# A hybrid encoder's beginning rebuilt: X loaded and turned by token blocks, parameters turned later

## What is computed

```
h    = x * rsqrt(mean(x*x) + eps) * g_mix_pre
proj = h @ w_in            # q1 q2 k1 k2 v lru_x lru_gate gate_attn gate_lru
lam  = exp(sum(lq1*lk1)) - exp(sum(lq2*lk2)) + lam_init      # used by the attention
a    = exp(-8 * r_gate * softplus(-lru_lambda))              # decay, used by the recurrence
```

## Time and profile before

| what | us |
|---|---|
| median of 3 runs | 2166.58 |
| lowest, highest | 2165.35, 2169.26 |
| the profiled execution, its own time | 2163.76 |
| its span, first to last instruction | 2161.6 |
| first row load issued, first product of the trio | 0.75, 39.41 |
| trio from, to | 39.41, 66.11 |

### The profile page before, as it was taken

How to read it: one execution, slowest core, us unless ns; L and a number is a source line. 1 busy time by engine, 2 the same in 40 slices (tenths; PEclk the granted TensorE clock), 3 DMA queues, 4 the chain that set the end, 5 groups by cost and what they waited for, 6 DMA issues and landing times.

```text
span 2161.6 us, 39635 instructions
## 1 busy us (share of the span) xinstructions
PE 2066.7 (96%) x15925; PEld 2013.3 (93%) x15925; DVE 1078.6 (50%) x2102; ACT 956.5 (44%) x1573; POOL 255.8 (12%) x283
## 2 busy tenths in 40 slices
PE   4999999999999899999989999999999989999997
PEld 4899999998999899999979999999999979999997
DVE  3366666665445432243455666666554363223434
ACT  4346464647235441233353656565652353312324
POOL 1303030200020220021012111111001102001200
PEclk9999999999999999999999999999999999999999
DMA  3313131312332223333322222222222323233332
GB/s 98 102 50 102 50 102 50 92 50 69 88 88 69 82 85 88 88 88 88 88 69 83 69 82 66 86 64 78 69 70 87 88 69 88 79 87 88 88 89 70
DMA packets 308155, 172.05 MB, mean 80 GB/s; under 512 B 7296, under 2 KB 303568, under 8 KB 308016
## 3 DMA queue, kind: packets, MB, share of 16 engines
q1 hardware_dynamic: 300720, 155.47, 24.9%
q0 software_dynamic: 7232, 14.49, 2.4%
q10 hardware_dynamic: 64, 0.13, 0.0%
HBM read 158.86 MB, written 11.21 MB: 79 GB/s over the span
## 4 chain that ended last, share of the span: by engine, by line
PE 81%; DVE 8%; ACT 7%; issue 3%; DMA 1%; ACTq 0%; DVEq 0%
PE PJ L529 60%; PE PJ L672 5%; PE PJ L541 4%; PE PX L698 3%; PE PX L736 3%; DVE w_lo L1356 2%; ACT w_hi L920 2%; PE PX L541 1%; DVE s L1558 1%; PE PX L546 1%; PE PX L714 1%; PE PX L624 1%; PE PX L692 1%; DVE uc L1595 1%; ACT L946 0%
## 5 line engine op out<-in xcount | busy, mean ns | idle before, releaser
L1356 DVE TENSOR_TENSOR w_lo<-w_raw,w_hi 128x1024 fp32r<-128x1024 f32 x288 | 385.5, 1351 | 360.7 <-ACT w_hi L920 360.1
L529 PE MATMUL PJ<-h_hi,w_hi 128*128 128x272 f32 x2304 | 491.0, 295 | 17.6 <-DVE w_lo L1356 16.7
L529 PE MATMUL PJ<-h_lo,w_hi 128*128 128x272 f32 x2304 | 475.9, 288 | 0.0
L529 PE MATMUL PJ<-h_hi,w_lo 128*128 128x272 f32 x2304 | 475.3, 288 | 0.0
L920 ACT ACTIVATE w_hi<-w_raw 128x1024 fp32r<-128x1024 f32 x288 | 298.4, 1047 | 209.8 <-DMA w_raw<-in_w_down 115.7
L529 PEld LDWEIGHTS PJ<-h_hi,w_hi 128*128 128x128 f32 x2304 | 362.9, 190 | 22.7 <-issue 12.4
L529 PEld LDWEIGHTS PJ<-h_hi,w_lo 128*128 128x128 f32 x2304 | 362.6, 189 | 0.0
L529 PEld LDWEIGHTS PJ<-h_lo,w_hi 128*128 128x128 f32 x2304 | 361.9, 189 | 0.0
L529 PE MATMUL PJ<-u_hi,w_hi 128*128 128x272 f32 x960 | 198.0, 288 | 3.4 <-DVE w_lo L1356 3.4
L529 PE MATMUL PJ<-u_lo,w_hi 128*128 128x272 f32 x960 | 197.8, 287 | 0.0
L529 PE MATMUL PJ<-u_hi,w_lo 128*128 128x272 f32 x960 | 197.3, 287 | 0.0
(11 more groups left out here) (293 smaller groups left out, 3761.9 us busy)
## 6 DMA issues: line engine op xcount, KB each, us to landing
w_raw<-in_w_in SPq DMA_DIRECT2D x112, 512.0 KB, 3.8
w_raw<-in_w_up SPq DMA_DIRECT2D x64, 512.0 KB, 4.0
w_raw<-in_w_down SPq DMA_DIRECT2D x64, 512.0 KB, 3.6
w_raw<-in_w_branch_attn SPq DMA_DIRECT2D x16, 512.0 KB, 3.6
w_raw<-in_w_branch_lru SPq DMA_DIRECT2D x16, 512.0 KB, 3.6
w_raw<-in_w_out SPq DMA_DIRECT2D x16, 512.0 KB, 3.6
out_prompt_k<-stage POOLq DMA_DIRECT2D x16, 256.0 KB, 2.8
out_prompt_v<-GA POOLq DMA_DIRECT2D x8, 512.0 KB, 3.9
```

Of the source, the lines that this page charges most:

```text
L529: mm = pe.matmul(PJ[:, buf, half, 0:HT], w[a], src[b][:, k0 + k, HT * half:HT * half + HT], start=first and k == 0 and a + b == 0, stop=en ...
L1356: dve.tensor_tensor(w_lo[:, n.slot, :, :], w_raw[:, n.slot, :, :], w_hi[:, n.hi, :, :].bitcast(F32), ALU.subtract).then_inc(w_lo_ready, 1)
```

## The change

- SP loads x_sample, blocks 1 and 2 of x_prompt (128 tokens each, 512 KB), weight tiles 0 and 1, blocks 3 and 4, weight tiles 2 and 3. Each block has its own semaphore.
- ACT's first load is the first norm's gain of layer 0, as 8 rows of 128 values, which PE turns by itself into `first_gain`; `h_chunk(0, ...)` and `h_rest(0, ...)` use that instead of `par`. ACT keeps four of the 13 row loads; the other nine move to POOL's queue, ahead of the fill of `w_gate` and of the lambda loads.
- PE turns X by token block: the sample block, block 1, the gain, block 2; blocks 3 and 4 inside the trio's first half, after k = 0 and k = 2; the parameter rows after k = 7. A block takes two PSUM banks; ACT copies one (feature tiles 0 to 3) into X, DVE the other.
- ACT loads the Exp table first. Splits of weight tiles, pieces of h and squares alternate, in the order in which the trio asks for them. The fourth split, the decay chain and the lambda products come behind h.
- POOL's first load of past keys waits for the last copy on DVE instead of for the last on ACT.
- The counts of `x_new` lose the 8 of the beginning; the rest of the kernel is the same.

```diff
 @@ SP
-            sp.dma_start(x_in[:, 1:5, :], A["x_prompt"][0].rearrange("(g t) d -> t g d", t=P)).then_inc(x_landed, 16)
+            for g in range(3):
+                load_x(g)
             for i in range(WR):
                 sp.dma_start(w_raw[:, i, :, :], pair_source(0, 0, i)).then_inc(w_landed[i], 16)
+                if i == 1:
+                    load_x(3)
+                    load_x(4)
 @@ POOL
+            for row, name in SMALL[4:]:
+                load_small(pool, row, name, small_landed)
+            for l in range(DEPTH):
+                pool.dma_start(rows[16 * l + R_CW:16 * l + R_CW + 4, :], A["conv_w"][l]).then_inc(small_landed, 16)
+                pool.dma_start(rows[16 * l + R_SC:16 * l + R_SC + 3, :], A["state_conv"][l, 0]).then_inc(small_landed, 16)
             pool.memset(w_gate[:], 0.0).then_inc(wg_zero, 1)
 @@ PE
+            def turn_x(g):
+                pe.wait_ge(x_landed[g], 16)
+                if g == 4:
+                    pe.wait_ge(x_in_dve, 1)
+                    pe.wait_ge(gain_ready, 1)
+                for b in range(2):
+                    for k in range(4):
+                        mm = pe.transpose(x_bank(g, b)[:, P * k:P * k + P], x_in[:, g, P * (4 * b + k):P * (4 * b + k) + P], ident[:])
+                    mm.then_inc(x_turned, 1)
+            def turn_par():
+                pe.wait_ge(par_landed, 16 * 4)
+                pe.wait_ge(small_landed, 16 * (5 + 2 * DEPTH))
+                pe.wait_ge(x_in_act, 4)
+                pe.wait_ge(x_in_dve, 5)
+                for k in range(KT):
+                    mm = pe.transpose(PX[:, 1, 32 * k:32 * k + 32], rows[0:32, P * k:P * k + P], ident[0:32, 0:32])
+                mm.then_inc(par_turned, 1)
 @@ PE, trio
+                        if S == 0 and h == 0 and k in (0, 2):
+                            turn_x(3 + k // 2)
+                        if S == 0 and h == 0 and k == KT - 1:
+                            turn_par()
+                        if S == 0 and h == 1 and k == 5:
+                            pe.wait_ge(par_step, 1)
 @@ PE, beginning
-            pe.wait_ge(par_landed, 16 * PAR_DMAS)
...
-            pe.wait_ge(x_new, KT)
+            pe.wait_ge(x_landed[0], 16)
...
+            turn_x(1)
+            pe.wait_ge(gain_landed, 16)
+            pe.transpose(PX[:, 1, 0:KT], gain_row[:], ident[0:KT, 0:KT]).then_inc(gain_turned, 1)
+            turn_x(2)
 @@ ACT, beginning
+            act.dma_start(gain_row[:], A["g_mix_pre"][0].rearrange("(k p) -> k p", p=P)).then_inc(gain_landed, 16)
+            for row, name in SMALL[:4]:
+                load_small(act, row, name, par_landed)
+            act.wait_ge(lam_step, 1)
+            load_table(ACT.Exp)
+            place_x(1)
+            place_x(2)
+            split_hi(pair_tile(0, 0, 0))
+            h_chunk(0, 0, 0)
+            h_chunk(0, 0, 1)
+            split_hi(pair_tile(0, 0, 1))
+            h_chunk(0, 0, 2)
+            place_x(3)
+            h_chunk(0, 0, 3)
+            h_chunk(0, 0, 4)
+            split_hi(pair_tile(0, 0, 2))
+            place_x(4)
+            x_chunk_square(0, 0)
...
+            act.wait_ge(par_step, 2)
             act.activation(lsc[:, 1, :], lsc[:, 0, :], ACT.Exp, scale=-1.0).then_inc(lam_act, 1)
+            split_hi(pair_tile(0, 0, 3))
+            for c in range(5):
+                x_chunk_square(1, c)
             act.wait_ge(lam_step, 4)
             act.activation(lsc[:, 7, 0:4], lsc[:, 6, 0:4], ACT.Exp).then_inc(lam_act, 1)
...
-            load_table(ACT.Ln)
-            for i in range(WR):
-                split_hi(pair_tile(0, 0, i))
 @@ DVE, beginning
+            place_x(0)
+            place_x(1)
+            dve.wait_ge(gain_turned, 1)
+            dve.tensor_copy(first_gain[:], PX[:, 1, 0:KT]).then_inc(gain_ready, 1)
+            place_x(2)
+            split_lo(pair_tile(0, 0, 0))
+            h_rest(0, 0, 0)
+            h_rest(0, 0, 1)
+            split_lo(pair_tile(0, 0, 1))
+            h_rest(0, 0, 2)
+            place_x(3)
+            h_rest(0, 0, 3)
+            h_rest(0, 0, 4)
+            place_x(4)
+            split_lo(pair_tile(0, 0, 2))
...
+            dve.wait_ge(par_turned, 1)
+            dve.tensor_copy(par[:], PX[:, 1, 0:256].rearrange("p (k r) -> p k r", r=32)).then_inc(par_step, 1)
...
+            split_lo(pair_tile(0, 0, 3))
             dve.wait_ge(lam_landed, 16 * 5 * DEPTH)
```

More of the change, by code:

```diff
@@ L275, in x_count @@
         def x_count(S):
[L277 removed]
+            return 10 * (S - 1)
         def x_whole(S):
[L281 removed]
+            return 10 * S
         def squares(l, s):
@@ L313, in proj, with pre_gain, x_bank, load_small @@
             return PJ[:, n.slot % 2, :, 0:HT]
+        def pre_gain(S, k):
+            return first_gain[:, k:k + 1] if S == 0 else gain(S // 2, k, R_MPRE if S % 2 else R_GPRE)
+        def x_bank(g, b):
+            return PX[:, b, :] if g == 4 else PX[:, 2 + b, :] if g == 3 else PJ[:, g - 1, b, :]
         def gain(l, k, row):
             return par[:, k, 16 * l + row:16 * l + row + 1]
+        SMALL = [(row, name) for row, name in (
+            (R_GPRE, "g_mix_pre"), (R_GPOST, "g_mix_post"), (R_MPRE, "g_mlp_pre"), (R_MPOST, "g_mlp_post"),
+            (R_CB, "conv_b"), (R_BR, "b_rg"), (R_BI, "b_ig"), (R_LAM, "lru_lambda"), (R_SL, "state_lru"))]
+        def load_small(eng, row, name, landed):
+            eng.dma_start(rows[row:row + 16 * (DEPTH - 1) + 1:16, :],
+                          A[name].rearrange("l o d -> (l o) d") if name == "state_lru" else A[name]).then_inc(landed, 16)
         def columns(name, l, block):
@@ L1173, in down_end, with place_x @@
                 f_square(l, 7, 0)
[L1176 to L1181, removed]
+            def place_x(g):
+                act.wait_ge(x_turned, 2 * g)
+                act.activation(X[:, 0:4, cols(g)], x_bank(g, 0).rearrange("p (k c) -> p k c", k=4), ACT.Copy).then_inc(x_in_act, 1)
@@ L1711, in _, with place_x @@
             dve.memset(dist_p[0:CHUNK, NP_ - CHUNK:NP_], NEG_DIST)
[L1713 to L1724, removed]
+            def place_x(g):
+                if g == 0:
+                    dve.wait_ge(x_turned, 1)
+                    dve.tensor_copy(X[:, :, 0:NS], PX[:, 0, 0:256].rearrange("p (k c) -> p k c", k=KT)).then_inc(x_in_dve, 1)
+                    return
+                dve.wait_ge(x_turned, 2 * g + 1)
+                dve.tensor_copy(X[:, 4:8, cols(g)], x_bank(g, 1).rearrange("p (k c) -> p k c", k=4)).then_inc(x_in_dve, 1)
+            place_x(0)
[13 more added lines that the diff above has]
+            split_lo(pair_tile(0, 0, 2))
+            h_rest(0, 1, 0)
+            h_rest(0, 1, 1)
+            h_rest(0, 1, 2)
+            h_rest(0, 1, 3)
             dve.wait_ge(par_turned, 1)
-            dve.tensor_copy(par[:], PX[:, 0, 0:256].rearrange("p (k r) -> p k r", r=32)).then_inc(par_step, 1)
+            dve.tensor_copy(par[:], PX[:, 1, 0:256].rearrange("p (k r) -> p k r", r=32)).then_inc(par_step, 1)
             dve.wait_ge(par_step, 1)
+            h_rest(0, 1, 4)
             for l in range(DEPTH):
@@ L1747, in _ @@
             dve.tensor_scalar(lsc[:, 2, :], lsc[:, 2, :], 0.0, None, ALU.max).then_inc(par_step, 1)
+            split_lo(pair_tile(0, 0, 3))
+            dve.wait_ge(lam_landed, 16 * 5 * DEPTH)
+            for l in range(DEPTH):
+                for j in range(2):
+                    i = dve.tensor_tensor_reduce(out=lprod[:], in0=lq[:, l, 2 * j, :], in1=lq[:, l, 2 * j + 1, :], scale=1.0, scalar=0.0,
+                                                 op0=ALU.mult, op1=ALU.add, accum_out=lsc[:, 6, 2 * l + j:2 * l + j + 1])
+                    if l == DEPTH - 1 and j == 1:
+                        i.then_inc(lam_step, 1)
+                    else:
+                        i.then_inc(lambda_chain, 1)
+                        dve.wait_ge(lambda_chain, 2 * l + j + 1)
+            for l in range(DEPTH):
+                dve.tensor_scalar(gs[:, l:l + 1], gs[:, l:l + 1], 1.0 - lam_init[l], None, ALU.mult)
             dve.wait_ge(lam_act, 1)
```

77 lines of the change are left out of this document (35 added, 42 removed).

## The result

| what | before | after |
|---|---|---|
| median, us | 2166.45 | 2144.52 |
| lowest, highest | 2165.35, 2169.26 | 2144.22, 2145.51 |
| profiled execution, own time | 2163.76 | 2144.52 |
| its span | 2161.6 | 2142.7 |
| trio from, to | 39.41, 66.11 | 13.16, 44.21 |

The changed kernel is faster: ratio 0.9898, 95% interval [0.988, 0.9915], 21.9 us by the medians. The forecast was 2145.0 us.

A forecast was written before the change was run, and what follows sets the result against it. PE's wait for thirteen row loads, then chained copies and splits, bounded the beginning. Trio's end from 66.1 to 44.5, 21.6 us less, gave 2142.2; with the 2.8 distance to the median, 2145.0 us; range 2140.5 to 2153.

The forecast's parts named there:

- The bound: Kernel's beginning: PE waits for all thirteen parameter row loads, until 20.93 us, not for X or the weights.
- Loads: Queues at start: bytes over measured pace plus 1.7 us; block 1 at 6.3, tile 1 at 12.0, no wait on SP.
- Until the second tile: Beginning, bounded by the chain of copies and splits: first product at 13.2 us, second tile's at 14.9.
- The trio: First three weight tiles: third stalls 0.3 us for VectorE; end at 44.5 instead of 66.1, 21.6 us less.
- Covers: Work under the trio's second half costs nothing: VectorE done near 40, lambda landed by about 24.7, PE asks at 44.5.
- Pieces paying one after another: Rival, start loads: each load pays its whole 3.8 us behind the one before; gain 16.0, 2150.6 us; chance 0.13.
- PE staying slow: Rival, trio's first half: fast product spacing comes only with the second half; gain 13.9, 2152.7 us; chance 0.11.
- Lambda too late: Rival, slower, before first rs product: lambda loads behind nine POOL loads cost from landing about 35; 62 gives 2171; chance 0.03.
- The path not shortened: Rival, trio: its length set by something keeping its time, as tiles 2 and 3 landing; gain below 4 us; chance 0.03.
- none of the gain is lost there: Stage behind the trio (66.11 to 78.58): waits counted from the trio's end, so the 21.6 us gain passes through.
- a sign of being wrong: Stages behind the trio: forecast wrong if they differ by more than 1 us, or if the trio ends after 53.
- The distance of span to median: Whole kernel: median 2166.58 stands 2.8 us above the profiled execution; kept, turning 2142.2 into 2145.0 us.

The follow-up runs named there:

- the trial: Changed kernel with the lambda and g_sub loads issued only when the trio's first half is done; 2144.58 us, ratio 0.9896.
- the disturbed landing above: Changed kernel unedited, measured and profiled a second time, its third weight tile landing at 22.49 us; 2146.34 us, ratio 0.9902.

## Why the prediction was right, and where its steps were not

**The bound.** That PE waited for the row loads and not for X or the weights holds as far as it goes: with that wait put back, the trio ends 7.4 us later. But a second wait stood 1 us behind it, which the prediction did not name: in the kernel before, the lambda loads landed at 19.7, and ACT's first copy of X waits for VectorE's work on them. With the rows alone moved that wait takes over and nothing is gained. The change moved both.

**Loads.** Predicted landings against measured: block 1 6.3 and 5.4, block 2 7.7 and 6.7, tile 0 9.8 and 10.3, tile 1 12.0 and 12.2. Bytes over the measured pace plus one latency came within 1 us of each. The rows, put at 19.2, landed at 12.6. **A step that failed:** SP, for which I took no wait, was held 4.04 us by the issue of block 3. The reason given, 0.3 MB ahead of the two tiles, was miscounted too: by the prediction's own sum the sample and two blocks are 1.18 MB. For block 3 the hold cost nothing, since it still landed at 13.6, ahead of PE's 15.52. But the tiles behind it on the queue were issued as much later, and the chain to the trio's end runs over this hold and the third tile's landing. How much sooner that tile would land without the hold was not tried.

**Until the second tile.** First product 13.2 and 13.16, second tile 14.9 and 14.64. The numbers held, the path only from tile 0's split on. That split was to begin at 10.3, right behind ScalarE's copy of block 2. The copy was through 1 us sooner (9.32), since the blocks landed sooner, and tile 0 landed 0.5 us later than predicted, so ACT waited 0.96 us for it and began at 10.28. The two errors cancelled, which is luck.

**The trio.** Block 4 turned by 21.0, measured 20.15; third tile 22.9 and 22.57; end 44.5 and 44.21. **Another step was wrong though its number came out:** I put the third tile's stall of 0.3 us on VectorE (copy 0.69 and split 1.22 after block 4). It was the tile's landing: 20.17, then 1.07 and 1.22, a stall of 0.57. VectorE was close behind: it was through with its copy 0.16 us before the split could begin, so alone it would have had the low part ready some 0.2 us sooner. I had worked out the landings of tiles 0 and 1 and never that of tile 2, and my rule would have given it too early, because the lambda and g_sub loads take a share of the DMA engines' time and SP's hold issued it later. The transposes of the parameters took 0.61, where I took 1.0 at their old pace.

**Covers.** VectorE reached the lambda products at 33.72 (33 predicted), and was through by 39 (40); the first rs product ran at 39.73, and PE asked at 44.21. Lambda landed at 21.8 (24.7). The point from which a late landing decides I put at 35, by 8.4 us of VectorE that contained its waits; without them it is 5.3, and the trial shows it at about 38.

**The rivals.** Pieces paying one after another: refuted by block 2 landing 1.3 us behind block 1, where 3.8 were needed, and by the load in one piece. No fixed cost per load is paid here piece behind piece. PE staying slow: not so, fast from 18.4 (predicted 19.4), but in the disturbed landing above it came back for fourteen products. Lambda too late: no. The path not shortened: no.

**The total.** The trio's end came 21.9 us sooner (21.6 predicted), the span fell by 18.9: by the step "none of the gain is lost there" 3.0 us were too much for this execution. The stages behind differ by more than the 1 us that the prediction named as a sign of being wrong. Of the 3.0, 1.4 lie in the longer stretch at 0.50, which the second execution of the same kernel does not have; for the rest the cause is open. The distance of span to median, which I kept at 2.8, vanished in about the same size and with the other sign, and the median came out right to 0.5 us by this luck; the second measurement's median is 1.3 us above the forecast. An error of 2.7 us would have stayed in the range, whose lower end is added up wrongly by half a us (2145.0 less 1 and 3 is 2141.0).

## What to carry to other kernels

When a beginning is set by one wait, undo its covers in the profile one after the other before counting: here the rows alone gave nothing, and a part is worth what the trio loses without it (11.2 us for the new order of splits and pieces) only while the other parts stand. Write down a landing for every transfer the first stage needs, the last one too, and count every other load that shares the queues by the time it takes and not by its bytes. A cover is measured in the engine's busy time behind the late transfer, without the waits it had in the old order.

## What the runs showed of the hardware that was not expected

- Small loads can cost far more than their bytes: with the eight lambda loads (32 KB each, replicated over 128 partitions) and the two of g_sub (0.5 KB each) in flight, all loads together moved 273 GB/s where they moved 349 without them (10 to 13 us), and 170 where they moved 262 (13 to 17 us), at the same DMA busy share.
- A load's issue can block: on SP 4.04 us for a block behind two weight tiles and 2.87 us for the last tile, against 0.41 to 0.76 for the other seven; 3.79 us on ACT for one row load.
- After a wait PE can start at the low level or fall to it later, and one kernel differs between executions: behind the trio, after 3.8 us of waiting, it worked at 0.50 for 6.1 us in the changed kernel's first profile and for 3.3 in its second; in the second, after a wait of 2.12 us ahead of the third tile, 0.50 came only 1.4 us after PE had started again.
- Transposes alone can bring the fast level, as one execution shows: with X in one piece PE had done nothing but transposes (11.4 to 15.5, 0.25 us apart) before its first three products, the last two 0.13 us apart; then it waited 1.33 us, and the next were 0.24 apart, at a granted clock of 0.50. In the changed kernel, after the same transposes and 3.63 us of waiting, the first products were 0.24 apart at once, and so they were with the lambda loads late, after 2.61 us. There the column of the granted clock reads 1.00: in that stretch the spacing tells the level and the column doesn't. The products of the kernel with X in one piece:

```profile
18.03 0.37 PE L573 MATMUL PJ<-h_hi,w_hi 128*128 128x288 f32 x1 [2.56 <-DVE h_lo L1431]
18.24 0.29 PE L573 MATMUL PJ<-h_lo,w_hi 128*128 128x288 f32 x1
18.37 0.29 PE L573 MATMUL PJ<-h_hi,w_lo 128*128 128x288 f32 x1
20.00 0.61 PE L573 MATMUL PJ<-h_hi,w_hi 128*128 128x288 f32 x1 [1.33 <-DVE w_lo L1425]
20.41 0.44 PE L573 MATMUL PJ<-h_lo,w_hi 128*128 128x288 f32 x1
20.64 0.44 PE L573 MATMUL PJ<-h_hi,w_lo 128*128 128x288 f32 x1
```
